# Even block of a two-layer diffusion backbone: input projections in three fp32r passes instead of one f32 pass

## What is computed

```python
h <- LN(a*h + 1/2*g_0*SwiGLU_a(mod_0(h)))            # ffn0 of the kernel
h <- LN(a*h + g_1*W_out[mixers(mod_1(h) W_in)])      # "even": neighbourhood attention | mLSTM
h <- LN(a*h + 1/2*g_2*SwiGLU_b(mod_2(h)))            # ffn1; then ffn2, odd, ffn3 for layer 1
```

## Time and profile before

| | us |
|---|---|
| median of 3 runs | 2009.19 |
| lowest and highest | 2009.07, 2010.22 |
| span of the profiled execution | 2008.5 |

### The profile page before, as it was taken

One profiled execution on the slowest core, in us unless ns is written; L12 is line 12 of the kernel. 1 busy time (PEld: TensorE's weight loads), 2 busy tenths in 40 slices (PEclk: granted clock), 3 DMA queues, 4 the chain that ended last, 5 costly groups with the idle time before them and its releaser, 6 DMA issues.

```text
span 2008.5 us, 24119 instructions
## 1 busy us (share of the span) xinstructions
PE 1905.3 (95%) x9168; PEld 1512.3 (75%) x9168; DVE 1263.0 (63%) x2217; ACT 648.5 (32%) x1102; POOL 290.2 (14%) x313
## 2 busy tenths in 40 slices
PE   5999999999998789899999989999999899989997
PEld 5888878884554455788887878888778866879997
DVE  7677777664864573877769367673777444464454
ACT  2322242323334441422224233222433232434453
POOL 0000001160000003400001131000044435130002
PEclk7999999999997899899999989999999999989999
DMA  9354545431440001454543233544134644204543
GB/s 363 123 199 182 190 161 153 146 120 61 177 179 0 1 0 43 158 198 175 206 175 144 87 155 132 204 172 177 48 134 176 252 179 152 89 38 168 196 157 108
DMA packets 43958, 290.10 MB, mean 144 GB/s; under 512 B 13916, under 2 KB 19676, under 8 KB 27232
## 3 DMA queue, kind: packets, MB, share of 16 engines
q1 hardware_dynamic: 35488, 271.13, 36.8%
q10 hardware_dynamic: 8384, 17.83, 2.3%
HBM read 272.16 MB, written 16.78 MB: 144 GB/s over the span
## 4 chain that ended last, share of the span: by engine, by line
PE 83%; DVE 9%; DMA 4%; ACT 3%; issue 1%; POOL 0%; SPq 0%; ACTq 0%; POOLq 0%; DVEq 0%
PE bank L623 13%; PE bank L628 13%; PE bank L625 13%; PE bank L680 6%; PE bank L689 6%; PE bank L686 6%; PE bank L810 4%; PE bank L807 3%; PE bank L794 3%; PE bank L989 2%; DMA slot<-in_down_dram 2%; PE bank L747 2%; DMA R<-in_ada_dram 1%; PE bank L737 1%; PE bank L986 1%; PE bank L944 1%
## 5 line engine op out<-in xcount | busy, mean ns | idle before, releaser
L1720 DVE CUSTOM_DVE_ANT_0 L<-slot 128x1024 f32<-128x1024 f32 x272 | 337.6, 1241 | 86.1 <-DMA slot<-in_ada_dram 79.0
L1173 ACT ACTIVATE w_hi<-slot 128x1024 fp32r<-128x1024 f32 x176 | 186.3, 1061 | 572.4 <-PE bank L628 561.2
L1777 DVE TENSOR_TENSOR w_lo<-slot,w_hi 128x1024 fp32r<-128x1024 f32 x176 | 216.8, 1234 | 206.6 <-ACT w_hi L1173 200.4
L623 PE MATMUL bank<-m_hi,w_hi 128*128 128x512 f32 (+1 forms) x1344 | 296.6, 363 | 3.2 <-ACT w_hi L1173 3.2
L628 PE MATMUL bank<-m_hi,w_lo 128*128 128x512 f32 (+1 forms) x1344 | 296.1, 362 | 0.0
L625 PE MATMUL bank<-m_lo,w_hi 128*128 128x512 f32 (+1 forms) x1344 | 296.1, 362 | 0.0
L623 PEld LDWEIGHTS bank<-m_hi,w_hi 128*128 128x128 f32 x1344 | 232.3, 189 | 43.1 <-ACT w_hi L1173 4.0
L628 PEld LDWEIGHTS bank<-m_hi,w_lo 128*128 128x128 f32 x1344 | 232.6, 189 | 39.3
L625 PEld LDWEIGHTS bank<-m_lo,w_hi 128*128 128x128 f32 x1344 | 232.6, 189 | 39.2
L1939 DVE TENSOR_TENSOR down_lo<-slot,down_hi 128x1408 fp32r<-128x1408 f32 x64 | 108.4, 1709 | 127.1 <-ACT down_hi L1223 126.8
L686 PE MATMUL bank<-g_lo,down_hi 128*128 128x512 f32 (+1 forms) x770 | 156.0, 351 | 0.1
(11 more groups left out here) (351 smaller groups left out, 2604.0 us busy)
## 6 DMA issues: line engine op xcount, KB each, us to landing
slot<-in_gateup_dram SPq DMA_DIRECT2D x44, 2048.0 KB, 8.0
slot<-in_ada_dram SPq DMA_DIRECT2D x34, 2048.0 KB, 8.1
slot<-in_down_dram SPq DMA_DIRECT2D x32, 1408.0 KB, 6.2
slot<-in_ev_in_dram SPq DMA_DIRECT2D x4, 2048.0 KB, 8.4
slot<-in_od_in_dram SPq DMA_DIRECT2D x4, 2048.0 KB, 9.2
R<-s_ops SPq DMA_DIRECT2D x16, 512.0 KB, 6.3
s_tables<-slot ACTq DMA_DIRECT2D x8, 768.0 KB, 3.3
R<-s_tables SPq DMA_DIRECT2D x8, 768.0 KB, 7.0
```

The costliest lines, as they stand in the source:

```text
L623: nc.tensor.matmul(bank[j][:, c0:T], w_hi[:, off, c, :], m_hi[:, c, c0:T], start=(c == 0), stop=False)
L1173: nc.scalar.activation(w_hi[:, off, :, :].rearrange("p a b -> p (a b)"), slots[b][:, (2 * (f % 2) + off) * D:(2 * (f % 2) + off + 1) * D], ...
L1720: ins = nc.vector.tensor_tensor_reduce(out=junk, in0=slots[k][:, t * D:(t + 1) * D], in1=csilu[s_], scale=1.0, scalar=0.0, op0=ALU.mult, o ...
L1777: nc.vector.tensor_tensor(w_lo[b][:, t, :, :].rearrange("p a b -> p (a b)"), slots[b][:, t * D:(t + 1) * D], w_hi[:, off, :, :].bitcast(F3 ...
```

## The change

All inputs and weights of the even block's input projections are split into rounded part and remainder, and every projection is three fp32r passes. Beside that:

- The four xm tiles' weights are loaded during ffn0's `down` (ahead of the load of tile d = 2) and split there, on ScalarE and VectorE, behind tiles 2 to 5 (`first_tile_hi`, `first_tile_lo`). `even` joins the stages whose inputs are split while the norm runs.
- Each later tile is one unit u of `PARTS` (gates among them). ScalarE rounds unit u + 2 when unit u is done (two buffers `part_hi`); VectorE makes the remainder in place in the slot (`part_rest`) for units 0 to 12, at fixed places of its stream; GpSimd makes it for units 13 to 20, the values (`values_rest`), behind waits for the local operators' DMAs. A value unit is a quarter of the contraction for all four token tiles.
- The S5 batches move: `OPERATORS_BEHIND` and `TURN_BEHIND` give the units behind which TensorE handles them.
- The weights alternate between slots 0 and 1; the gates' are in slot 3. The attention bias is loaded into slot 2 after the even block's third weight load and is masked in place by GpSimd. Attention's values are in slot 0, so one half of the output weights is loaded when attention is done.

Unchanged lines that the rest needs: VectorE's scans stand between `dve.wait_ge(sem("even_soft"), 2)` and `nc.vector.tensor_scalar(rows[:, 4:6, :] ...)`; ScalarE's `soft_rows` is the old Silu, Exp, Ln sequence.

```diff
-EVEN_LOADS = [(0, "ev_in", 0, SLOT), (1, "ev_gates", None, KT * 4 * HEADS), (3, "ev_in", 1, SLOT), (2, "ev_in", 2, SLOT),
-              (0, "ev_in", 3, SLOT), (1, "ev_v", 0, SLOT), (2, "ev_v", 1, SLOT), (3, "ml_qk", None, 2 * WIDTH),
-              (0, "ev_out", 0, SLOT), (1, "ev_out", 1, SLOT)]
+EVEN_LOADS = [(0, "ev_in", 0, SLOT), (3, "ev_gates", None, KT * 4 * HEADS), (1, "ev_in", 1, SLOT), (0, "ev_in", 2, SLOT),
+              (1, "ev_in", 3, SLOT), (0, "ev_v", 0, SLOT), (1, "ev_v", 1, SLOT), (3, "ml_qk", None, 2 * WIDTH),
+              (1, "ev_out", 1, SLOT), (0, "ev_out", 0, SLOT)]
+PARTS = ([("zo", 1, j) for j in range(2)] + [("gates", 3, 0)] + [("zo", 1, j) for j in range(2, 4)] + [("q", 0, j) for j in range(4)]
+         + [("k", 1, j) for j in range(4)] + [("na_v", 0, j) for j in range(4)] + [("ml_v", 1, j) for j in range(4)])
+FIRST_PARTS = 4
+TURN_BEHIND = {4: 0, 5: 1, 8: 2, 10: 3, 12: 4, 13: 5, 15: 6, 17: 7}
+OPERATORS_BEHIND = {7: 0, 9: 1, 11: 2, 12: 3, 14: 4, 16: 5, 17: 6, 19: 7}
+REST_BEFORE = {0: (7,), 1: (8, 9), 2: (10, 11), 3: (12,)}
+VALUES_AT = 13
...
+        even_m_hi = rounded("even_m_hi", R_at, 13312, [P, KT, T])
+        first_hi = rounded("first_hi", slots_at[2], 0, [P, 4, KT, P])
+        part_hi = rounded("part_hi", R_at, 10240, [P, 2, KT, P])
+        gate_lo = rounded("gate_lo", slots_at[3], 1024 + KT * 16, [P, KT, P])
...
+                    if d == 2 and s == 0:
+                        load(0, i["ev_in"][0])
+                        loads[0] += 1
...
                     for n, (k, src, at, width) in enumerate(EVEN_LOADS):
-                        if n == 1:
+                        if n == 0:
+                            continue
+                        if n == 2:
                             sp.wait_ge(sem("r_ready"), before("r_ready", "ffn0") + KT)
+                        if n == len(EVEN_LOADS) - 1:
+                            sp.wait_ge(sem("even_y0"), 8)
+                        load(k, i[src] if at is None else i[src][at], width=width, at=1024 if src == "ev_gates" else 0)
+                        loads[k] += 1
                         if n == 3:
-                            sp.wait_ge(sem("na_bias_masked"), 8)
-                        load(k, i[src] if at is None else i[src][at], width=width)
-                        loads[k] += 1
+                            bias_loads()
...
+            def first_tiles():
+                take(0)
+                late = 3
+                for s_ in range(2):
+                    a, b = STREAMS[s_]
+                    lo = lambda j, c: nc.tensor.matmul(banks[j][:, a:b], first_hi[:, j, c, :], m_lo[:, c, a:b], start=False, stop=(c == KT - 1))
+                    for c in range(KT):
+                        pe.wait_ge(sem("m_ready"), before_m("even", s_) + c + 1)
+                        for j in range(4):
+                            if s_ == 0 and c == 0:
+                                pe.wait_ge(sem("part_lo_ready"), j + 1)
+                            nc.tensor.matmul(banks[j][:, a:b], first_hi[:, j, c, :], even_m_hi[:, c, a:b], start=(c == 0), stop=False)
+                            nc.tensor.matmul(banks[j][:, a:b], w_lo[0][:, j, c, :], even_m_hi[:, c, a:b], start=False, stop=False)
+                        if c >= late:
+                            pe.wait_ge(sem("m_lo_ready"), before_lo("even", s_) + c - late + 1)
+                            for j in range(4):
+                                lo(j, c - late)
+                    for c in range(KT - late, KT):
+                        pe.wait_ge(sem("m_lo_ready"), before_lo("even", s_) + c + 1)
+                        for j in range(4):
+                            last = lo(j, c)
+                            if c == KT - 1 and s_ == 1:
+                                last.then_inc(used[0] if j == 3 else sem("even_proj_done"), 1)
...
+            def even_tile(u, n, bank):
+                what, k, j = PARTS[u]
+                w_rest = gate_lo if what == "gates" else w_lo[k][:, j, :, :]
+                if j == 0:
+                    take(k)
+                if n is not None and n >= 4:
+                    pe.wait_ge(sem("even_proj_read"), n - 3)
+                pe.wait_ge(sem("part_hi_ready"), FIRST_PARTS + u + 1)
+                for c in range(KT):
+                    nc.tensor.matmul(bank, part_hi[:, u % 2, c, :], even_m_hi[:, c, :], start=(c == 0), stop=False)
+                for c in range(KT):
+                    nc.tensor.matmul(bank, part_hi[:, u % 2, c, :], m_lo[:, c, :], start=False, stop=False)
+                pe.wait_ge(sem("part_lo_ready"), FIRST_PARTS + u + 1)
+                for c in range(KT):
+                    last = nc.tensor.matmul(bank, w_rest[:, c, :], even_m_hi[:, c, :], start=False, stop=(c == KT - 1))
+                last.then_inc(used[k] if j == 3 or what == "gates" else sem("even_proj_done"), 1)
...
+            def even_values(u, n):
+                what, k, q = PARTS[u]
+                hi = part_hi[:, u % 2, :, :].rearrange("p (c a) b -> p c (a b)", c=2)
+                rest_ = w_lo[k][:, q, :, :].rearrange("p (c a) b -> p c (a b)", c=2)
+                tokens = lambda v, c, j: v[:, 2 * q + c, j * P:(j + 1) * P]
+                if q == 0:
+                    take(k)
+                pe.wait_ge(sem("part_hi_ready"), FIRST_PARTS + u + 1)
                 for j in range(4):
+                    if q == 0:
+                        pe.wait_ge(sem("even_proj_read"), n + j - 3)
+                    for c in range(2):
+                        nc.tensor.matmul(banks[j][:, :], tokens(even_m_hi, c, j), hi[:, c, :], start=(q == 0 and c == 0), stop=False)
+                        nc.tensor.matmul(banks[j][:, :], tokens(m_lo, c, j), hi[:, c, :], start=False, stop=False)
+                pe.wait_ge(sem("values_lo_ready"), u - VALUES_AT + 1)
+                for j in range(4):
+                    for c in range(2):
+                        last = nc.tensor.matmul(banks[j][:, :], tokens(even_m_hi, c, j), rest_[:, c, :], start=False, stop=(q == 3 and c == 1))
+                    if q == 3:
+                        last.then_inc(used[k] if j == 3 else sem("even_proj_done"), 1)
+                    elif j == 3:
+                        last.then_inc(sem("even_quarter_done"), 1)
...
+                first_tiles()
+                n = 4
+                for u, (what, k, j) in enumerate(PARTS):
+                    if what == "gates":
+                        even_tile(u, None, banks[4][:, :])
+                    elif what in ("na_v", "ml_v"):
+                        even_values(u, n)
+                        n += 4 if j == 3 else 0
+                    else:
+                        even_tile(u, n, banks[n % 4][:, :])
+                        n += 1
+                    if u in OPERATORS_BEHIND:
+                        s5_operators(OPERATORS_BEHIND[u])
+                    if u in TURN_BEHIND:
+                        if u == 4:
+                            pe.wait_ge(sem("even_rows_ready"), 4)
+                        turn_raw(TURN_BEHIND[u])
...
+            def first_tile_hi(j):
+                if j == 0:
+                    act.wait_ge(used[2], uses_before("even")[2])
+                    act.wait_ge(full[0], 16 * (uses_before("even")[0] + 1))
+                nc.scalar.activation(first_hi[:, j, :, :].rearrange("p a b -> p (a b)"), slots[0][:, j * D:(j + 1) * D], ACT.Copy).then_inc(sem("part_hi_ready"), 1)
...
+                    if name == "ffn0" and 2 <= d < 6:
+                        first_tile_hi(d - 2)
...
+                def next_hi(u):
+                    if u + 2 < len(PARTS):
+                        part_hi_of(u + 2)
+                part_hi_of(0)
+                part_hi_of(1)
...
+                quarters, n = 0, 4
+                for u, (what, k, j) in enumerate(PARTS):
+                    if what == "gates":
+                        slot_done[3] += 1
+                        act.wait_ge(used[3], slot_done[3])
+                        next_hi(u)
+                        gate_rows()
+                    elif what in ("na_v", "ml_v"):
+                        if j < 3:
+                            quarters += 1
+                            act.wait_ge(sem("even_quarter_done"), quarters)
+                            next_hi(u)
...
+                        if n == 12:
+                            act.wait_ge(sem("even_rows_step"), 3)
+                            nc.scalar.activation(rows[:, 2:4, :], rows[:, 2:4, :], ACT.Exp)
+                        projected("even", n, k)
+                        next_hi(u)
+                        src = banks[n % 4][:, :]
+                        if what == "zo":
+                            nc.scalar.activation(sig_o[:, j, :], src, ACT.Sigmoid).then_inc(read, 1)
+                            if j == 3:
+                                soft_rows()
...
+                part_rest(0)
+                part_rest(1)
+                convolve(0)
+                convolve(1)
+                part_rest(2)
```

(43 more changed lines are left out.)

219 lines of the change are left out of this document (102 added, 117 removed).

## The result

The changed kernel takes 2014.83 us (median of 7 runs, 2013.97 to 2019.89), the kernel before beside it on the same chip 2009.65 (2009.07 to 2012.38): a ratio of 1.0027, 95% interval 1.0018 to 1.0036. It is slower by a quarter of a per cent, where 2001.7 was forecast and slower had a chance of 0.07. The profiled execution spans 2012.2 us, against 2008.5.

The account below looks back on a forecast made before the run. TensorE was taken to bound the kernel, with 83% of the chain. The terms −30.4 − 3.3 + 11.9 + 2.4 + 1.2 + 4.3 + 4.0 + 2.4 = −7.5 us gave a 2001.0 span and 2001.7 median, range 1997 to 2006.

Parts of the forecast that it names:

- The saving: Even block's projections on TensorE: twenty tiles and the gates' tile at 5.43 us instead of 6.88, saving 30.4 us.
- The first four tiles: The xm tiles at the even block's start: 24.3 us instead of 27.6, a saving of 3.3 us.
- The stall at unit 6: q's second tile: TensorE waits 11.9 us for VectorE's remainder, queued behind the mLSTM scans.
- slow clock: Behind the idle stretch at unit 6, dense work runs at the 1.2 GHz level at first, costing 2.4 us.
- The load in ffn0: Down tile 2 waits 4.0 us behind the 2 MB load moved ahead of its own, plus 2.4 us of clock.
- The other moves cost nothing: Remaining moved loads (gates, zo, bias, late output weights) arrive in time or under cover, at no cost.
- the term for that remainder: Unit 18: TensorE waits 1.2 us for GpSimd's remainder, which stands behind the third local write.
- The end of the block: Behind the last S5 batch TensorE idles 5.1 us where there was 0.8, costing 4.3 us.
- the second rival: VectorE becomes the bound, stopped by GpSimd's eight remainders (+6 us, 2007.7), or lags in batches 0 to 3; chance 0.12.
- The slower case: Between unit 6 and the block's end the 1.2 GHz level persists, giving 2014 us; chance 0.07.

Follow-up runs that it names:

- e1: Changed kernel with the 2 MB load of the first even weights issued behind, not ahead of, down tile 2's load in ffn0: 2008.49 us.
- e2: Changed kernel with the second value weights' and query/key weights' loads held until batch 5's raw S5 blocks have landed: 2015.07 us.
- e3: Changed kernel with the load of the output weights' second half held until the last local S5 write has landed: 2008.85 us.
- e6: Changed kernel with the eight value remainders made by VectorE instead of GpSimd: 2012.37 us.
- e11: Changed kernel with ffn0, raw-block and last-write loads reordered, VectorE's order mended, and GpSimd's unit 18 remainder ahead of the third-write wait: 1993.74 us.
- e5: Changed kernel with VectorE's remainder 6 and S5 batch 0 ahead of the softplus wait, and remainder 7 between the scans: 2010.67 us.
- e10: As e9, with GpSimd's eight bias masks held until the S5 blocks of batch 2 are built: 1995.91 us.
- e12: As e9, with the eight bias masks made by VectorE behind the last S5 batch instead of by GpSimd: 1984.42 us.
- e4: Changed kernel with only unit 6's remainder put ahead of VectorE's wait for the softplus and the scans: 2013.46 us.
- e9: Changed kernel with the e1, e2, e3 and e5 edits, value remainders on VectorE, and remainders 7 and 8 moved earlier still: 1990.26 us.

## Why the prediction was wrong

The span was to be 2001.0 and is 2012.2. By the prediction's own steps:

- **The saving.** Groups of eight passes start 1.81 us apart and a unit takes 5.43 us, as forecast, but behind S5 work its first group takes 1.93 (485.39 to 487.32 above): 14 of the 21 units take 5.55, 1.7 us that the sum left out. The first four tiles took 24.9 us (427.39 to 452.25). The 24.3 forecast began with 0.5 for a late start; from the same point on, 0.45 us ahead of the first pass, it is 25.3, so 1.0 was left out.
- **The stall at unit 6.** 11.67 us against 11.9, ended by VectorE's remainder, and 2.1 us of slow clock against 2.4. Right in place, cause and size.
- **The load in ffn0.** The 4.0 of waiting and 2.4 of clock were right: tile 2 starts 4.0 us late, and by 341.69 it is 6.6. The end of the down tiles is 7.5 us late. The other 0.9 come from an xm remainder ahead of a split, which the text allowed for ("at most 1 us") and costed at nothing; e1 still has 0.8 of it.
- **The other moves cost nothing.** This step failed. The text took the S5 batches' loads to be as they were, and looked only at when the moved loads are needed, not at what is queued behind them. `ev_v` 1 is now issued at 546.35, with 512 KB behind it, some 3 us ahead of batch 5's raw blocks, the last of which took 8.5 us instead of 2.7: 3.45 us of idle TensorE. e2 shows that this gap alone is worth nothing, since the remainder of unit 18 waits just beneath: with the gap mended, 1.33 and 2.21 us of waiting stand in its place; the term for that remainder (1.2, measured 0.31) looked right only because TensorE came 3.45 us late, though a remainder on GpSimd took 2.4 us and not the 2.9 assumed. Together with the 0.50 us at batch 7, the three are 4.3 us where 1.2 stood in the sum.
- **The end of the block.** This step failed, and it is the largest. The chain was right (last batch, copies, sum, write, four banks), and one term in it was mis-sized: the write at 2.5 us, from the earlier trace rows, where the queue was idle. `ev_out` 1 now goes to slot 1, which comes free when unit 20 ends, so its 2 MB are issued 0.26 us ahead of the write, which takes 8.1. e3 takes just this away and gets 4.97 us, against 5.1 forecast. Had the sum priced the 2 MB, as it did in ffn0 at 4.9 us, it would have come to 2006.6.
- **VectorE stands still for GpSimd's remainders** (the second rival). Its mechanism is right, its price is not. The forecast took the half rate of the earlier trace rows. The Trainium skill's rule (SBUF — State Buffer, section SBUF: two separate sides), that the two engines shut each other out for a whole instruction, is what the trace shows: 2.1 to 2.2 us for each remainder of 2.4, and e6 takes them away with their cause. But 17 us of stops beside about as much slack cost TensorE 0.5 us, and e11 says the same. The masks were priced only as a bound of the stall at unit 6. They are eight GpSimd instructions with two inputs, harmless in the changed kernel, where VectorE is idle for 11 us behind them, 3.5 us of the wait in e5, and the bound in e10.
- **The slower case** was put on the clock lasting long. It did not: TensorE went on at 500.98, and from 506 the granted clock was 1.00. What took the time from the forecast to slower was for the most part the write at the end: with that alone mended (e3) the time is 2008.85, level with the kernel before. Mending the raw blocks' gap alone (e2) gains nothing.

The terms that can be set against the 11.2 us: 5.7 at the end, 3.1 at batch 5 and units 18 and 19 (e2 has much the same in other places), 1.7 in the units, 1.1 in the down tiles, 1.0 in the first tiles, less 0.5 at unit 6 and 1.0 that comes back behind the block (620.02 to the end is 1392.2 us, where 615.30 to the end was 1393.2): in all 11.1.

The question was where 34 us of saved TensorE time went. The answer of e12: for the most part into the order of work on SyncE, VectorE and GpSimd, and into what GpSimd did beside VectorE; mending both brings 26.7 of the 34. With the same arithmetic, TensorE's two waits of 11.67 and 3.45 us are gone, the end waits 5.02 instead of 10.80, and the time is 1984.42 against 2011.08 for the kernel before in the same rounds.

## What to carry to other kernels

When loads are re-dealt to buffers, price each moved load by what is issued right behind it on any queue, not only by when its own data are wanted. Taking a remainder out of one engine's queue shows the next one in it: before mending an order, list every wait that stands within a few us beneath the one removed. Work for GpSimd beside a busy VectorE is not free capacity; put it where VectorE is idle, or give it to VectorE, which did the masks in half the time.

## What the runs showed of the hardware

- A small transfer behind a 2 MB load on another engine's queue: a 256 KB write 0.26 us behind it took 8.1 us, against 2.4 (e3: 2.4 again), and a 128 KB read 3.2 us behind it, with 512 KB more in between, 8.5 us, against 2.7 (e2: 2.6).
- On one queue the loads of 2 MB and 1.4 MB in ffn0 landed in the order of issue: at 324.2 and 327.6 us, and with the order turned (e1) at 322.7 and 327.6.
- A VectorE instruction with two inputs in SBUF and a GpSimd one with two did not overlap. Eight of eight GpSimd remainders (2.34 to 2.51 us) lengthened a VectorE group by 2.1 to 2.2 us; eight masks stopped VectorE for some 7.4 us in two groups of e10; and VectorE held up one mask by 3.3 us in the changed kernel.
- The granted clock is not told by the length of the last gap. It stayed at 1.00 behind gaps of 3.45 us (the changed kernel), 3.29 (e4) and 3.16 (e1), and fell (0.50 to 0.71 over the next 4 us) behind 3.60 (e3), 3.18 (e6) and 3.11 (e5) at the same place, and elsewhere behind 1.82 us in e9 and 1.71 in e4. Each fall cost 1.6 to 3.3 us. What decides is left open; it makes the price of a gap of 2 or 3 us uncertain by as much again.
